# Down stage of an encoder block: x1 and the factor rows in 256 KB pieces, another place for the three-product steps' sum, and a tail by token block

## The chip, the cores and the metric

The kernel runs on one core of one Trainium2 chip. The metric is the device time of one execution in microseconds. Lower is better.

## The reference

One encoder block over 512 tokens and 2048 features, in float32, with a conditioning vector that gives a shift, a scale and a gate for each half:

```
mod = silu(c) @ w_ada + b_ada                    # sh1, sc1, gt1, sh2, sc2, gt2
h = rmsnorm(x, g_norm1) * (1 + sc1) + sh1
x1 = x + gt1 * hybrid_mixer(h, ...)              # mLSTM heads and windowed attention
h = rmsnorm(x1, g_norm2) * (1 + sc2) + sh2
x2 = x1 + gt2 * ((silu(h @ w_gate) * (h @ w_up)) @ w_down)     # FF = 5632
out = rmsnorm(x2, g_final)
```

## The kernel before

Every large product is done as three TensorE passes: a weight tile and an activation tile are each split into an upper part (ScalarE copies it to the rounded type) and a lower part (VectorE subtracts the upper part from the whole), and a product is upper by upper, upper by lower, lower by upper. For each 128x1024 weight tile there is therefore one ScalarE operation, one VectorE operation and 12 matmuls of 512 columns, called an entry. The upper and lower tiles have four buffers (`EHI`, `ELO`), so ScalarE may make the upper part of entry e only when TensorE has finished entry e-4 (`u_used`).

The matrix products of the feed-forward part are done in a seven-product scheme over 2x2 blocks (P1 to P7), which needs sums of weight blocks (VectorE, L1834 in the units, L1975 in the Down stage) and sums of activation blocks.

**The ten middle units.** A unit (u = 1 to 10, 28 entries each) multiplies the next chunk of w_gate and w_up. Beside it the activation of the chunk before is turned by TensorE (`turn_a`), combined by VectorE (`combine_a`, `low_a1`, `low_sums`) and stored to HBM by ScalarE's DMA queue (`turned`, `split_sums`, `keep_sums`, `keep_lows`), to be loaded again in the Down stage: the unsplit parts in `a_keep`, the split pairs in `a_pair`. ScalarE and VectorE work through an order written out by hand: the number in `if e == 14:` is the entry after whose upper or lower part the step stands. TensorE's entry 17 waits for the first four of the middle sums (`middle_y`, L1909, and `middle_zw`, L1918).

**The Down stage.** 44 steps: 11 row chunks of w_down for the near columns' P1, P5, P6, P4 (steps 0 to 10, four products a step), 11 for their P7, P2, P3 (steps 11 to 21, three products), and the same for the other half of the columns (22 to 32, 33 to 43). A step loads 4 or 3 tiles of 512 KB of w_down, 1 MB of pairs (`down_pairs`) and 512 or 256 KB of unsplit blocks (`down_blocks`), all from SyncE's queue. The loads of step s wait for the last lower part of step s-2, the pairs for TensorE's last use of the pairs of step s-2, the blocks for VectorE's `block_lo` of step s-2. `sums_after(e)` says which weight sums stand behind the lower part of entry e on VectorE.

x1, kept in HBM since the middle of the kernel, comes back in pieces (`xp`), is turned by TensorE behind the entries of steps 12 to 19 (`turn_x1`), and copied to `x2`. The gate's factors gt2 are turned to a row (`gain_row`), stored and loaded back for all partitions (`gtb`); `gfb` is the final gain. What the products give is multiplied by the factors and added to x2 (`pre_scale`, `pre_add`, `join_late`, and for the last products `take` and `join_x1`). The tail is the final norm: squares summed by ScalarE (`x2_squares`), mean by VectorE (`final_mean`), power -0.5 by GpSimd (`final_rs`), scaling of half the columns on ScalarE and half on VectorE (`scaled_out`), and four outputs of 1 MB, one for each block of 128 tokens, in the order 2, 3, 0, 1.

Of the kernel before, what the change touches and what calls it, by code (L numbers as in the profile page):

```python
# [34 lines left out]
F32 = mybir.dt.float32  # L35
# [64 lines left out]
def program(nc, x, c, positions, w_ada, b_ada, g1, g2, w_in, b_gates, w_conv, b_conv, gm, sink, ga,  # L100
            w_out, w_gate, w_up, w_down, gf, rope_inv, out, x1_keep, a_keep, a_pair, gt_keep):
    ctx = ExitStack()
    with ctx:
# [142 lines left out]
        gt16 = at("gt16", [KT, P], F32, mix + 28 * S * 4)  # L246
# [57 lines left out]
        sh_ok, sl_ok = gate_sb, gate_sel  # L304
        H0, V0 = 48, 256
# [68 lines left out]
        def sums_after(e):  # L374

            due = [(s, name, FIRST_E[s] + i - 2 + (s == 2) + (s == STEPS - 1))
# [56 lines left out]
        def _(sp):  # L433
# [164 lines left out]
            def x1_piece(cb):  # L598

                if cb >= 2:  # L600
                    sp.wait_ge(xT_ps, 16 + 4 * cb - 4)
                sp.dma_start(xp[cb % 2][:], x1_keep[:, 4 * cb:4 * cb + 4, :]).then_inc(xs_ld[cb % 2], 16)
# [3 lines left out]
            for s in range(STEPS):  # L606
# [23 lines left out]
        def _(pool):  # L630
# [56 lines left out]
            def final_rs(h):  # L687
                pool.wait_ge(n_ms, 1 + h + 1)
                two = slice(2 - 2 * h, 4 - 2 * h)
                pool.tensor_tensor(rs[:, two], ve[:, two], halfneg[:, two], ALU.pow).then_inc(n_rs, 1)  # L690

            final_rs(0)
            final_rs(1)
# [3 lines left out]
        def _(act):  # L697
# [395 lines left out]

            def split_sums(u, rows):

                act.wait_ge(sl_ok, 3 * u - 1)
                act.dma_start(a_pair[rows, 2:8:5, :], a1_lo[:].bitcast(F32)).then_inc(at_st[0], 16)
# [1644 lines left out]
```

## Time and profile before

| | us |
|---|---|
| median of 3 runs (2301.48 to 2304.58) | 2304.0 |
| the profiled execution | 2300.64 |
| its span | 2298.8 |
| TensorE busy, 96% of the span | 2198.7 |
| VectorE busy, 75% | 1729.3 |
| ScalarE busy, 41% | 951.4 |
| GpSimd busy, 9% | 209.3 |

The span is what the trace covers; the execution's own time is 1.8 us above it. Positions below are microseconds from the span's start. The units run from about 1022 to 1812, the Down stage from there to the end. Busy time of TensorE is the time in which a matmul is under way, and matmuls overlap, so a matmul's own duration (0.39 us) is not its pitch.

### The profile page before, as it was taken

To read this page: it belongs to the slowest core of one execution; us is meant where nothing else is said; L and a number is where in the kernel's file an instruction comes from. 1 tells how busy PE (TensorE), PEld (TensorE's weight loads), DVE (VectorE), ACT (ScalarE), POOL (GpSimd) and SP (SyncE) were. 2 spreads that over 40 slices of the span, in tenths; PEclk is the share of its full clock that TensorE was granted. 3 is DMA by queue.
4 is the path that set the end of the run, shared out by engine and by line. 5 is a ranking of instruction groups with operands and counts; after the bars stand their busy time and mean duration, and the time that the engine had idled before them with its cause. 6 is when DMAs were issued, how large, how long until landed. Compare 5 with 4: busy or idle time off the path is not lost.

```text
span 2298.8 us, 27658 instructions
## 1 busy us (share of the span) xinstructions
PE 2198.7 (96%) x10119; PEld 1813.8 (79%) x10119; DVE 1729.3 (75%) x2017; ACT 951.4 (41%) x1231; POOL 209.3 (9%) x72
## 2 busy tenths in 40 slices
PE   5999999999999999999999999999999979999996
PEld 5878878888877788788888888888888768778874
DVE  5978657474766766668887888788888878579976
ACT  4333232323346212454444444444444444455533
POOL 0002333333320013000000000000000000000000
PEclk7999999999999999999999999999999989999998
DMA  9943434344541767225544545544554699999885
GB/s 360 379 155 120 166 129 156 139 162 166 183 160 43 274 259 273 92 101 179 170 169 159 174 169 177 173 160 160 173 178 169 251 369 325 333 317 364 309 297 219
DMA packets 219082, 477.60 MB, mean 208 GB/s; under 512 B 14928, under 2 KB 60272, under 8 KB 202864
## 3 DMA queue, kind: packets, MB, share of 16 engines
q1 hardware_dynamic: 200656, 440.06, 54.4%
q10 hardware_dynamic: 18336, 36.33, 4.2%
q8 instruction: 58, 0.95, 0.2%
q14 instruction: 32, 0.26, 0.0%
HBM read 436.22 MB, written 40.12 MB: 207 GB/s over the span
## 4 chain that ended last, share of the span: by engine, by line
PE 69%; DVE 12%; DMA 7%; issue 5%; ACT 4%; SPq 1%; POOL 1%; ACTq 1%; DVEq 0%; POOLq 0%
PE ps L2162 20%; PE ps L2164 20%; PE ps L2163 20%; DMA wraw<-in_w_down 6%; ACT whi L1044 2%; DVE wraw L1975 1%; PE ps L2319 1%; DVE wlo L1964 1%; DVE acc L1322 1%; PE ps L2332 1%; DVE d_hl L2038 1%; PE ps L2330 1%; PE ps L2253 1%; DMA araw<-in_w_ada 1%; DVE wlo L1815 1%
## 5 line engine op out<-in xcount | busy, mean ns | idle before, releaser
L1044 ACT ACTIVATE whi<-wraw 128x1024 fp32r<-128x1024 f32 x200 | 209.5, 1058 | 226.5 <-DVE wraw L1834 155.3
L1815 DVE TENSOR_TENSOR wlo<-wraw,whi 128x1024 fp32r<-128x1024 f32 x200 | 240.4, 1218 | 63.9 <-ACT whi L1044 63.9
L2162 PE MATMUL ps<-whi,d_hl 128*128 128x512 f32 x616 | 243.6, 395 | 30.6 <-DVE wlo L1964 13.7
L2162 PE MATMUL ps<-h_hi,whi 128*128 128x512 f32 x680 | 272.5, 401 | 0.0
L2164 PE MATMUL ps<-h_hi,wlo 128*128 128x512 f32 x680 | 267.4, 393 | 0.0
L2163 PE MATMUL ps<-h_lo,whi 128*128 128x512 f32 x680 | 267.0, 393 | 0.0
L2162 PE MATMUL ps<-whi,sk_hi 128*128 128x512 f32 x640 | 250.7, 392 | 0.0
L2164 PE MATMUL ps<-whi,sk_lo 128*128 128x512 f32 x640 | 249.2, 389 | 0.0
L2163 PE MATMUL ps<-wlo,sk_hi 128*128 128x512 f32 x640 | 249.1, 389 | 0.0
L2164 PE MATMUL ps<-whi,d_hl 128*128 128x512 f32 x616 | 241.3, 392 | 0.0
L2163 PE MATMUL ps<-wlo,d_hl 128*128 128x512 f32 x616 | 241.1, 391 | 0.0
L2162 PE MATMUL ps<-whi,q_hi 128*128 128x512 f32 x572 | 223.7, 391 | 8.6 <-DVE vg L1918 7.5
L2164 PE MATMUL ps<-whi,q_lo 128*128 128x512 f32 x572 | 222.6, 389 | 0.0
L2163 PE MATMUL ps<-wlo,q_hi 128*128 128x512 f32 x572 | 222.6, 389 | 0.0
L652 POOL TENSOR_TENSOR wlo<-wraw,whi 128x2048 fp32r<-128x2048 f32 x34 | 159.3, 4686 | 441.8 <-ACT whi L746 441.8
L746 ACT ACTIVATE whi<-wraw 128x2048 fp32r<-128x2048 f32 x38 | 72.6, 1911 | 247.1 <-PE ps L2164 247.1
L2162 PEld LDWEIGHTS ps<-whi,d_hl 128*128 128x128 f32 x616 | 116.5, 189 | 60.6 <-issue 21.3
L1559 DVE SCALAR_TENSOR_TENSOR acc<-araw,csil,acc 128x2048 f32<-128x2048 f32 x60 | 159.6, 2660 | 5.1 <-DMA araw<-in_w_ada 2.8
L1044 ACT ACTIVATE whi<-araw 128x1024 fp32r<-128x1024 f32 x80 | 84.7, 1059 | 180.6 <-DVE araw L1834 155.7
L1159 ACT ACTIVATE whi<-wraw 128x1024 fp32r<-128x1024 f32 x88 | 93.2, 1060 | 157.0 <-DVE wraw L1975 99.1
L2164 PEld LDWEIGHTS ps<-h_hi,wlo 128*128 128x128 f32 x680 | 129.0, 190 | 27.5
L2162 PEld LDWEIGHTS ps<-h_hi,whi 128*128 128x128 f32 x680 | 129.7, 191 | 26.1 <-issue 0.8
(363 smaller groups left out, 4120.8 us busy)
## 6 DMA issues: line engine op xcount, KB each, us to landing
araw<-in_w_ada SPq DMA_DIRECT2D x64, 1024.0 KB, 6.2
wraw<-in_w_gate SPq DMA_DIRECT2D x88, 512.0 KB, 3.9
wraw<-in_w_up SPq DMA_DIRECT2D x88, 512.0 KB, 4.7
wraw<-in_w_down SPq DMA_DIRECT2D x88, 512.0 KB, 5.8
d_hl<-a_pair SPq DMA_DIRECT2D x44, 1024.0 KB, 9.2
wraw<-in_w_in SPq DMA_DIRECT2D x38, 1024.0 KB, 5.3
acc<-in_w_down SPq DMA_DIRECT2D x44, 512.0 KB, 7.2
acc<-in_w_up SPq DMA_DIRECT2D x40, 512.0 KB, 5.5
```

The source lines that it names most:

```text
L652: pool.tensor_tensor(xlo[par][:], xraw[par][:], xhi[par][:].bitcast(F32), ALU.subtract)\
L746: A(xhi[par][:], xraw[par][:], ACT.Copy).then_inc(whi_ok, 1)
L1044: A(EHI[e % 4], src, ACT.Copy).then_inc(uhi_ok, 1)
L1159: A(EHI[e % 4], DRAW[s % 2][D_RAW[name]], ACT.Copy).then_inc(uhi_ok, 1)
L1322: V_.scalar_tensor_tensor(out=acc[:, half], in0=slot, scalar=csil[:, kt:kt + 1], in1=acc[:, half], op0=ALU.mult, op1=ALU.add).then_inc(ada ...
L1559: V_.scalar_tensor_tensor(out=acc[:], in0=araw[par][:], scalar=csil[:, kt:kt + 1], in1=acc[:], op0=ALU.mult, op1=ALU.add).then_inc(ada_acc, 1)
L1815: V_.tensor_tensor(ELO[e % 4], src, EHI[e % 4].bitcast(F32), ALU.subtract).then_inc(ulo_ok, 1)
L1964: V_.tensor_tensor(ELO[e % 4], DRAW[s % 2][D_RAW[name]], EHI[e % 4].bitcast(F32), ALU.subtract)\
L1975: V_.tensor_tensor(DRAW[s % 2][i], DRAW[s % 2][i], other, ALU.add).then_inc(usum_ok, 1)
L2162: pe.matmul(o, w_hi, m_hi, start=first, stop=False)
L2163: pe.matmul(o, w_hi, m_lo, start=False, stop=False)
L2164: return pe.matmul(o, w_lo, m_hi, start=False, stop=last)
```

## The change

1. **x1.** The four 1 MB pieces become 16 tiles of 256 KB, spread over the steps (`X1_AT`), with three `xp` buffers in place of two.
2. **Factor row and final gain.** The factors are stored straight from `mod` by ScalarE's queue, ahead of the first unit, column by column; TensorE's transpose and ScalarE's copy (`gain_row`) go. Both rows are loaded in quarters over the steps (`GT_AT`, `GF_AT`).
3. **Three-product steps.** The sum for P7 stands one entry later, behind the last lower part of the step before. The last two steps' order is P7, P7, P2, P2, P3, P3 in place of P7, P2, P7, P2, P3, P3.
4. **Units.** `split_sums` stands behind entry 13 in place of 14, without the store of a1's lower part; that store (`keep_low_a1`) and `keep_sums` stand behind entry 14, `keep_lows` behind 15 in place of 16, and `low_sums` on VectorE behind 14 in place of 15.
5. **Tail.** Joins, mean, power and scaling go by token block; two scalings stand between the joins. The gains of the first half (`gain`) stand in steps 32 to 35 in place of 39 to 42. `block_lo(0)` stands behind the first sums.

```diff
@@ buffers and semaphores
-        xp = [at(f"xp{i}", [P, 4, S], F32, mix + i * 8192) for i in range(2)]
+        xp = [at(f"xp{i}", [P, 4, S], F32, mix + o) for i, o in enumerate((0, 8192, 49152))]
+        x1_ld = [(xs_ld[0], 32), (xs_ld[1], 32), (ada_ld[0], 224), (ada_ld[1], 224)]
@@ down_order, sums_after
-                return [(s + i, p) for ps_ in (("P7", "P2"), ("P3",)) for i in range(2) for p in ps_] if s == STEPS - 2 else []
+                return [(s + i, p) for ps_ in (("P7",), ("P2",), ("P3",)) for i in range(2) for p in ps_] if s == STEPS - 2 else []
-            due = [(s, name, FIRST_E[s] + i - 2 + (s == 2) + (s == STEPS - 1))
+            due = [(s, name, FIRST_E[s] + i - 2 + (s == 2) + down_step(s)[1])
@@ sync
+            def x1_tile(kt):
+
+                cb, (ready, _) = kt // 4, x1_ld[kt // 4]
+                if kt == 12:
+                    sp.wait_ge(xT_ps, 16 + 4)
+                sp.dma_start(xp[cb % 3][:, kt % 4, :], x1_keep[:, kt, :]).then_inc(ready, 16)
+
+            def rows_of(dst, row, ready, quarter):
+
+                part = slice(quarter * S, quarter * S + S)
+                sp.dma_start(dst[:, part], row[part].partition_broadcast(P)).then_inc(ready, 16)
+
+            X1_AT = {2: (0,), 3: (1,), 4: (2, 3), 5: (4,), 6: (5,), 7: (6, 7), 8: (8,), 9: (9,), 10: (10, 11),
+                     16: (12, 13), 17: (14, 15)}
+            GT_AT, GF_AT = (11, 12, 22, 23), (24, 25, 26, 27)
...
                     sp.wait_ge(u_used, 28 * NU)
-                    sp.dma_start(gfb[:], gf.partition_broadcast(P)).then_inc(x_ld[0], 16)
-                    x1_piece(0)
-                    x1_piece(1)
-                if s == NCH + 4:
+                for kt in X1_AT.get(s, ()):
+                    x1_tile(kt)
+                if s in GT_AT:
                     sp.wait_ge(c_ld, 16 + 16)
-                    sp.dma_start(gtb[:], gt_keep.rearrange("a b -> (a b)").partition_broadcast(P)).then_inc(wg_ld, 16)
-                    x1_piece(2)
-                if s == NCH + 6:
-                    x1_piece(3)
+                    rows_of(gtb, gains_row, wg_ld, GT_AT.index(s))
+                if s in GF_AT:
+                    rows_of(gfb, gf, x_ld[0], GF_AT.index(s))
@@ scalar, the units
                         if e == 13:
                             keep_x(u)
+                            split_sums(u, rows)
                         if e == 14:
-                            split_sums(u, rows)
+                            keep_low_a1(u, rows)
+                            keep_sums(u, rows)
                         if e == 15:
-                            keep_sums(u, rows)
-                        if e == 16:
                             keep_lows(u, rows)
 
+            act.wait_ge(modp_ok, 8)
+            act.dma_start(gt_keep.rearrange("a b -> b a"), mod[:, 5, :], allow_slow_non_contiguous=True).then_inc(c_ld, 16)
             unit(1, slice(0, P))
@@ scalar, the tail
+            square(2, 2, 5, 8)
+            square(2, 3, 6, 9)
+            square(3, 2, 7, 10)
+            square(3, 3, 8, 11)
+            scaled_out(0, 2)
+            square(0, 2, 9, 12)
+            scaled_out(1, 3)
+            square(1, 2, 10, 13)
+            square(0, 3, 11, 14)
+            square(1, 3, 12, 15)
+            scaled_out(2, 0)
+            scaled_out(3, 1)
@@ vector, the units
-                        if e == 15:
+                        if e == 14:
                             low_sums(u)
@@ vector, the Down stage and the tail
-                    if e == FIRST_E[3 * NCH + 6 + i]:
+                    if e == FIRST_E[2 * NCH + 10 + i]:
                         gain(i)
...
+            take(0, 0, 1)
+            take(1, 0, 2)
+            take(0, 1, 3)
+            final_mean(2, 2)
+            take(1, 1, 4)
+            dve.wait_ge(x_ld[0], 16 + 64)
+            scaled_out(0, 2)
+            take(2, 0, 5)
+            final_mean(3, 4)
+            take(2, 1, 6)
+            scaled_out(1, 3)
+            take(3, 0, 7)
+            take(3, 1, 8)
+            final_mean(0, 7)
+            final_mean(1, 8)
+            scaled_out(2, 0)
+            scaled_out(3, 1)
@@ tensor
-            def gain_row():
-
-                pe.wait_ge(mix_ok, 6)
-                pe.transpose(ps[6][0:KT, 0:P], mod[:, 5, :], ident[:]).then_inc(cst_T, 1)
-
```

In the new tail `take(i, b, n)` multiplies one block's 512 columns out of PSUM by the factors and adds them to x2 (two VectorE operations), and `square`, `final_mean` and `final_rs` take one block.

## Rows read from the trace of the kernel before

**Rows 1.** TensorE's waits, units (1040 to 1812): line waited for, us in total, times, longest.

```profile
PE ps L2162 <- DVE vg L1918: 7.5, 9, 1.3
```

**Rows 2.** TensorE's waits, Down stage (1790 to 2299).

```profile
PE ps L2162 <- DVE wlo L1964: 13.7, 10, 2.4
PE ps L2162 <- DVE d_hl L2038: 12.6, 1, 12.6
PE ps L2162 <- DMA d_hl<-a_pair: 2.1, 1, 2.1
```

**Rows 3.** Windows: length, busy of PE, PEld, DVE, ACT, POOL, PEclk, DMA share, GB/s.

```profile
1858.00:1862.00 4.00, 3.96 (x9) 3.17 (x10) 4.00 (x4) 0.00 (x0) 0.00 (x0) 0.50 0.93 316
2080.00:2140.00 60.00, 60.00 (x266) 49.71 (x265) 58.61 (x53) 33.19 (x41) 0.00 (x0) 1.00 0.96 356
2210.00:2260.00 50.00, 42.96 (x184) 34.10 (x185) 34.45 (x33) 18.69 (x22) 0.00 (x0) 1.00 0.86 293
```

**Rows 4.** Timeline of VectorE, 1846 to 1858: start, us, engine, line, operation.

```profile
1848.25 0.68 DVE L1864 TENSOR_TENSOR s_lo<-sA,vg_hi 128x512 fp32r<-128x512 f32 x1
1855.62 1.22 DVE L1975 TENSOR_TENSOR wraw<-wraw 128x1024 f32<-128x1024 f32 x1 [6.69 <-DMA wraw<-in_w_down]
```

**Rows 5.** Timeline of TensorE, 1858 to 1862.

```profile
1858.04 0.80 PE L2162 MATMUL ps<-whi,d_hl 128*128 128x512 f32 x1 [12.61 <-DVE d_hl L2038]
```

**Rows 6.** DMA view, 1826 to 1860.

```profile
DMA packets 4456, 12.69 MB, mean 373 GB/s; under 512 B 335, under 2 KB 335, under 8 KB 3817
```

**Rows 7.** Timeline of ScalarE, 1815 to 1866.

```profile
1842.81 0.64 ACT L1100 ACTIVATE vg_hi<-stT 128x512 fp32r<-128x512 f32 x1 [7.16 <-DMA a_pair<-vg_hi]
```

**Rows 8.** Chain that ended last, 2239 to 2250: start, us, what.

```profile
2239.89 6.58 DMA wraw<-in_w_down
...
2246.57 1.23 DVE wraw L1975
2247.80 0.60 DVE d_hl L2038
2248.40 1.14 DVE wlo L1964
```

**Rows 9.** DMA issues of the whole span: count, KB each, median us to landing.

```profile
out<-x SPq DMA_DIRECT2D x4, 1024.0 KB, 6.3
...
wgraw<-in_w_in SPq DMA_DIRECT2D x1, 128.0 KB, 7.6
```

**Rows 10.** Timeline of TensorE, its last matmul.

```profile
2280.48 0.39 PE L2164 MATMUL ps<-whi,d_hl 128*128 128x512 f32 x1
```

**Rows 11.** Timeline of VectorE, the tail.

```profile
2283.35 0.69 DVE L2079 TENSOR_TENSOR x<-x,c 128x512 f32<-128x512 f32 x1
...
2285.10 4.87 DVE L2092 SCALAR_TENSOR_TENSOR x<-x,tiny,gfb 128x1024 f32<-128x1024 f32 x4
```

**Rows 12.** Timeline of SyncE, the tail.

```profile
2286.47 4.11 SPq L625 DMA_DIRECT2D out<-x  x4
```

**Rows 13.** Timeline of ScalarE, one unit (1205 to 1240), entries 14 to 16.

```profile
1212.20 1.06 ACT L1044 ACTIVATE whi<-araw 128x1024 fp32r<-128x1024 f32 x1 [0.69 <-PE ps L2164]
...
1215.49 0.63 ACT L1100 ACTIVATE vg_hi<-stT 128x512 fp32r<-128x512 f32 x1 [2.23 <-DVE a_lo L1856]
...
1217.37 1.06 ACT L1044 ACTIVATE whi<-wraw 128x1024 fp32r<-128x1024 f32 x1 [0.72 <-ACT vg_hi L1101]
...
1221.54 0.34 ACTq L1109 DMA_DIRECT2D a_pair<-s_lo  x1
```

**Rows 14.** Timeline of VectorE, the same unit.

```profile
1213.56 1.22 DVE L1856 TENSOR_TENSOR a_lo<-stT,vg_hi 128x1024 fp32r<-128x1024 f32 x1
...
1218.46 1.23 DVE L1815 TENSOR_TENSOR wlo<-wraw,whi 128x1024 fp32r<-128x1024 f32 x1 [2.54 <-ACT whi L1044]
...
1220.81 1.22 DVE L1815 TENSOR_TENSOR wlo<-wraw,whi 128x1024 fp32r<-128x1024 f32 x1
...
1227.76 1.28 DVE L1918 TENSOR_TENSOR vg<-ps,u2b 128x512 f32<-128x512 f32 x2
```

**Rows 15.** Timeline of TensorE, the same unit, entry 17.

```profile
1229.17 0.49 PE L2162 MATMUL ps<-whi,q_hi 128*128 128x512 f32 x1 [0.78 <-DVE vg L1918]
```

More of the change, by code:

```diff
@@ L685, in _, with final_rs @@
             pool.tensor_tensor(rs, ve, halfneg, ALU.pow).then_inc(n_rs, 1)
[L687 to L693, printed above, removed]
+            def final_rs(n, tb):
+                pool.wait_ge(n_ms, 1 + n + 1)
+                pool.tensor_tensor(rs[:, tb:tb + 1], ve[:, tb:tb + 1], halfneg[:, tb:tb + 1], ALU.pow).then_inc(n_rs, 1)
+            for n, tb in enumerate((2, 3, 0, 1)):
+                final_rs(n, tb)
         @block.scalar
@@ L1190, in x1_turned, with square, x2_squares, scaled_out @@
                 A(x2[:, g % 4, g // 4 * S:(g // 4 + 1) * S], ps[6 + g % 2][:], ACT.Copy).then_inc(xT_sb, 1)
-            def x2_squares(n, i, halves=(0, 1)):
-                h, c = ((1, 0), (1, 1), (0, 0), (0, 1))[i]
-                for b in halves:
-                    act.wait_ge(x2_ok, 4 * n + i + 1 + (b if n and i == 3 else 0))
-                    if n or i or b:
-                        act.wait_ge(ssq_ok, TB + 8 * n + 2 * i + b)
-                    tb, cb = 2 * h + b, 2 * n + c
-                    A(vg[:, 0, :], x2[:, tb, cb * S:(cb + 1) * S], ACT.Square, accum_out=ssq4[:, tb, cb:cb + 1])\
-                        .then_inc(ssq_ok, 1)
-            def scaled_out(h):
-                act.wait_ge(n_rs, 1 + h + 1)
+            def square(tb, cb, ready, done):
+                act.wait_ge(x2_ok, ready)
+                if done:
+                    act.wait_ge(ssq_ok, TB + done)
+                A(vg[:, 0, :], x2[:, tb, cb * S:(cb + 1) * S], ACT.Square, accum_out=ssq4[:, tb, cb:cb + 1])\
+                    .then_inc(ssq_ok, 1)
+            def x2_squares(i):
+                h, c = ((1, 0), (1, 1), (0, 0), (0, 1))[i]
+                for b in range(2):
+                    square(2 * h + b, c, i + 1, 2 * i + b)
+            def scaled_out(n, tb):
+                act.wait_ge(n_rs, 1 + n + 1)
                 act.wait_ge(z_ok, 4)
-                for tb in (2 - 2 * h, 3 - 2 * h):
-                    A(x2[:, tb, 0:2 * S], x2[:, tb, 0:2 * S], ACT.Copy, scale=rs[:, tb:tb + 1]).then_inc(y_ok[0], 1)
+                A(x2[:, tb, 0:2 * S], x2[:, tb, 0:2 * S], ACT.Copy, scale=rs[:, tb:tb + 1]).then_inc(y_ok[0], 1)
             block_hi(0)
@@ L1224, in _ @@
                 if e == 10:
+                    keep_low_a1(NCH, slice(NU * P, NCH * P))
                     keep_sums(NCH, slice(NU * P, NCH * P))
@@ L1243, in _ @@
                     if e == END_E[2 * NCH + 2 * i + 2]:
-                        x2_squares(0, i)
-            for i in range(3):
-                x2_squares(1, i)
-            x2_squares(1, 3)
-            scaled_out(0)
-            scaled_out(1)
+                        x2_squares(i)
+            square(2, 2, 5, 8)
[10 more added lines that the diff above has]
+            scaled_out(3, 1)
         @block.vector
@@ L2054, in gain, with take @@
                 if i == 0:
-                    dve.wait_ge(x_ld[0], 16 + 16)
+                    dve.wait_ge(x_ld[0], 16 + 32)
                 V_.tensor_tensor(x2_part(0, h, c), x2_part(0, h, c), both(gfb[:, c * S:(c + 1) * S]), ALU.mult)\
                     .then_inc(z_ok, 1)
-            def take(i, b=None):
+            def take(i, b, n):
                 name, c, t = (("P7", 0, tmp[0]), ("P7", 1, tmp[1]), ("P2", 0, kept), ("P3", 1, left))[i]
-                if b is None:
-                    dve.wait_ge(u_used, E0 + end_of(1, name))
-                    if i == 0:
-                        dve.wait_ge(pre_ok, 14)
-                for k in (range(2) if b is None else (b,)):
-                    last = V_.tensor_tensor(t[:, k, :], ps[DBANK[1][name] + k][:], gains(1, c), ALU.mult)
-                last.then_inc(t_ok, 1)
@@ L2088, in scaled_out @@
-            def scaled_out(h):
-                dve.wait_ge(n_rs, 1 + h + 1)
-                for tb in (2 - 2 * h, 3 - 2 * h):
-                    V_.scalar_tensor_tensor(out=x2[:, tb, 2 * S:], in0=x2[:, tb, 2 * S:], scalar=rs[:, tb:tb + 1],
-                                            in1=gfb[:, 2 * S:], op0=ALU.mult, op1=ALU.mult).then_inc(y_ok[1], 1)
-            block_lo(0)
+                dve.wait_ge(u_used, E0 + end_of(1, name) + (b if name == "P3" else 0))
+                V_.tensor_tensor(t[:, b, :], ps[DBANK[1][name] + b][:], gains(1, c), ALU.mult).then_inc(t_ok, 1)
```

69 lines of the change are left out of this document (22 added, 47 removed).

## Prediction

> **What bounds the kernel now.** I read the waits of TensorE first, because it is the engine that works nearly all the time, and split them at the end of the ten middle units. In the units TensorE waits 7.5 us in nine equal small waits, always for the same VectorE line L1918 [rows 1]. In the Down stage it waits 13.7 us in ten pieces for lower weight parts (L1964), once 12.6 us for a block's lower part (L2038), and once 2.1 us for a transfer of pairs [rows 2]. Next the windows: the four-product stretch has no idle time at all, with the DMA engines 0.96 busy; the second three-product stretch loses 7 of 50 us [rows 3]. 60 us for 266 matmuls gives 2.71 us for an entry of 12 matmuls: 10.85 us for a four-product step, 8.1 us for a three-product step. So TensorE bounds the kernel, and only an added or removed wait of TensorE, or the tail after it, can move the time. The timelines then say how each wait comes about.
>
> **The start of the Down stage: about 7.5 us less.** At step 2 SyncE queues the final gain and two x1 pieces, 3 x 1.05 MB, ahead of step 3's loads. VectorE, free at 1848.9, waits until 1855.6 for those loads (first sum of step 3), and L2038, which stands behind that sum in VectorE's order, releases TensorE at 1858.0 [rows 4, 5]. The change leaves 0.26 MB there: 2.88 MB less at the 373 GB/s of this stretch [rows 6] is 7.7 us. But VectorE can't be earlier than 1848.9, so the wait falls by 6.7 us. It doesn't go to nothing: ScalarE stood 7.2 us for its own store until 1842.8 [rows 7], VectorE's place follows from that, and the store still shares the DMA engines. Should the store land sooner, up to 3 us more come back; should it hold all up, 3 us less. After the long wait TensorE restarts at a granted clock of 0.50, the lower of its two levels (1.2 GHz): 9 matmuls in 4 us, where full clock gives 17.7 at 266 in 60 us [rows 3]; the 8.7 that lack are 2.0 us. I count 0.8 us of that as saved (0 to 2). Range 4 to 11.
>
> Afterwards the pieces must fit into the steps. A four-product step loads 3.67 MB (9.8 us at 373 GB/s, of 10.85): 1.0 us is free, a piece takes 0.7 us. Two pieces in one step (steps 4, 7, 10) take 1.4 us and lean on the next one. The factor and gain rows, one quarter a step, go by the same sum. I count 0.
>
> Here the Trainium skill speaks against the change: "DMA: Bandwidth & Descriptors", section Bandwidth, Measured, says to batch DMAs to 1 MiB or more and gives 2.0 us plus bytes over 436 GB/s each. By it 18 more transfers cost 36 us of DMA time. The trace agrees only for a transfer that stands alone; queued 512 KB loads moved at 373 GB/s in the mean. By the row the sum has 0 for it.
>
> **Three-product steps: 13.7 us less.** The chain there is a loop: load 6.58 us, sum 1.23 us, block's lower part 0.60, lower part of the last product 1.15, issue of the next load: 9.6 to 10 us for a step of 8.1 [rows 8]. The cause is that the sum of step s+1 stands ahead of the last lower part of step s, which releases the loads of s+2. With the sum behind it, the loads go out about one landing earlier. The new loop: after the last lower part come sum 1.2, upper part 1.1 and lower part 1.15 us, against a need three entries later; about 4 us of room. Bandwidth: 2.88 MB a step is 7.7 us at 373 GB/s, under 8.1. So all ten waits [rows 2] go. Bound: if bandwidth holds at two thirds, 9 us. VectorE gets the gains of L2056 in steps 32 to 35 too, beside the mixing; step 33 then holds some 10 us of its work against 8.1, with about 5 us of lead before it. I take 0, bound 2 us of loss.
>
> **The last two steps: 1.1 us less.** Both P7 now go first, so step 43's pairs are needed two entries (5.4 us) after they are issued, before three. A 1 MB transfer alone lands in 6.3 us [rows 9]; now they stand behind late loads, then they will not. Wait 1.0 in place of 2.1 us; bounds 0 and 4. The gain row's transpose and its TensorE wait disappear, 0.3 us.
>
> **The tail: 1.9 us less.** Now TensorE ends at 2280.9 and the span at 2298.8, 17.9 us [rows 10]. VectorE ends its joins 3.2 us after TensorE, and then four scalings take 4.87 us [rows 11]; the four outputs are issued from 2286.5 to 2290.6 and 4.2 MB drain in a row [rows 12]. After: from the last P7 until TensorE's end are 10.9 us; VectorE starts its block work 2.4 us into them (last upper and lower part) and has 16 half operations of 0.69, two scalings of 1.2 and two means of 0.35: free 5.5 us after TensorE. Square 0.85, mean 0.35, power up to 1.7, last scaling 1.2: last output issued 9.6 us after TensorE, landing 6.3 us later: 16.0 us. Blocks 2 and 3 are out by then. Bounds 0 and 4.
>
> **The ten units: 17.4 us more.** The diff also moves three things in every unit, which its name doesn't tell. Follow one unit. Now: the upper part of entry 14 starts at 1212.20, right when TensorE allows; then ScalarE waits for L1856 (1213.56, ends 1214.8), issues a store, makes two copies from 1215.49 and starts entry 15's upper part at 1217.37 [rows 13]. Its lower part is at 1218.46, the two sums' lower parts behind it, entry 16's lower part at 1220.81, and from there without a gap the weight sum, entry 17, the middle sums, L1918 at 1227.76 [rows 14]; TensorE starts entry 17 at 1229.17, 0.78 late [rows 15]. After: the copies stand between entry 13 and 14. They still need L1856 (the buffer is shared), so ScalarE stands until 1214.9, and entry 14's upper part starts 1.88 us (1217.37 less 1215.49) later, 1216.8. Its lower part: 1.09 us later, 1217.9. The sums' lower parts now stand behind it, until 1220.25 (2.35 from one part to the next but one, as 1218.46 to 1220.81). ScalarE must see these before it issues the last two stores, which stand ahead of entry 16's upper part. The stores now end at 1221.9, 1.07 us behind their release, then 0.2: entry 16's upper part at 1221.5, its lower part at 1222.6. That is 1.8 us later than 1220.81, and all that follows is back to back up to L1918. TensorE's own time doesn't move, so the wait is 0.78 + 1.8 = 2.6 us. Entries 14 to 16 themselves are due at 1220.3, 1223.0 and 1225.7 (2.71 each before 1228.4) and have their lower parts by 1219.1, 1221.4 and 1223.7. Nine waits of 0.83 become 2.6: 15.9 us; unit 1 has none now and some room, 1.5 us. The queues passed: three stores of 0.5 us stand ahead of entry 15's upper part, in its room. Bounds: 0, if the stores cost ScalarE nothing and the order resolves itself; 22, if entry 16 is late as well.
>
> **The factor row's store.** It goes out column by column, 2048 single values, ahead of unit 1, where ScalarE waits for its first load anyway. The nearest row has 2048 runs of 64 bytes: 7.6 us to landing among other loads [rows 9]. It may delay the first loads of unit 1. TensorE is there still busy with the entries of the stage before. I take 0, bound 3 us. The same page of the Trainium skill (section Latency and other measured facts) says that a last dimension that isn't contiguous gives one descriptor per element; no run here shows its price for 4 bytes.
>
> **Sum.** -7.5 - 13.7 - 1.1 - 0.3 - 1.9 + 17.4 = -7.1 us: 2293.5 against the profiled execution's 2300.6, whose span is 2298.8. The median of the runs is 2304.0, 3.4 us above it, so 2296.9 on the scale of the runs.
>
> **Rivals.** (a) The units don't slow: ScalarE's issue of stores overlaps, entry 16 is in time. Then -24.5: 2279.5. For it: the stores' own landing is close to L1918 as well and gets 0.5 us earlier. Against: each dependency above is written in the code. (b) The three-product steps stay bound by transfers: 355 GB/s wanted against 373. The ten waits stay or shift to the pairs: +6.6, 2310. Against: 0.96 busy without a wait in the four-product stretch [rows 3]. (c) Each small piece costs the DMA engines a fixed time: 6.3 us for 1 MB less 2.8 us of moving is 3.5 us. 12 pieces in steps 2 to 10 are 42 us against 9 free: +33, less 7: about 2330. It decides from 1.0 us a piece on. Its rule is the page's rule on batching. (d) The wait at the start remains, since ScalarE's store and not the queue holds it: -0.4: 2303.6.
>
> **How the numbers follow.** Forecast 0.60 (its own range 2290 to 2303), (a) 0.15, (b) 0.12, (c) 0.05, (d) 0.08. A measurement tells 0.2%, 4.6 us, from no change: faster is below 2299.4, slower above 2308.6. Of the forecast's 0.60, 0.43 are faster, 0.15 within, 0.02 slower; (a) is faster; (b) 0.05 within and 0.07 slower; (c) slower; (d) 0.06 within, 0.01 each side. Faster 0.59, same 0.26, slower 0.15. The range 2284 to 2307 leaves out most of (a), and (c) with a part of (b).
>
> **What would show it.** The wait for L1918 should read about 2.6 us in each unit and each unit 1.8 us longer. The wait for L2038 should be near 6 us, those for L1964 in the Down stage gone, the tail near 16 us, and the DMA share in the three-product steps above 0.9. A unit wait still at 0.8, or waits for loads in steps 4 to 10, makes the prediction wrong.

## The result, and the profile after

| | before | after |
|---|---|---|
| median of 13 runs each, in turns on one chip | 2303.6 us (2297.9 to 2307.7) | 2310.3 us (2305.0 to 2316.5) |
| ratio, 95% interval | | 1.0031 (1.0021 to 1.0041) |
| profiled execution | 2300.6 us | 2313.3 us |
| its span | 2298.8 us | 2311.5 us |
| its mean granted clock | 0.979 | 0.976 |

The forecast was 2296.9 us and faster; the kernel is slower, by 6.7 us in the medians and outside the range of 2284 to 2307. The two profiled executions lie 12.7 us apart, because before's is 3 us under its median and after's 3 us over. The sums below are made between these two executions; what a single edit is worth on the scale of the runs is read from the experiments.

TensorE's waits after the change, in the ten units (1040 to 1832) and in the Down stage (1800 to 2312), answer to [rows 1] and [rows 2]. The first view:

```profile
PE ps L2167 <- DVE vg L1933: 25.0, 10, 2.6
```

The second:

```profile
PE ps L2167 <- DVE d_hl L2053: 4.2, 1, 4.2
...
PE ps L2167 <- DMA d_hl<-a_pair: 2.0, 1, 2.0
```

L1933 is L1918 of before, L2053 is L2038. The unit waits have grown from 7.5 to 25.0 us. In the Down stage the long wait has gone from 12.6 to 4.2 us, and the ten waits for L1964 are no longer there. The wait for the pairs is what it was.

Windows of after (columns as in [rows 3]). The first lies in the three-product steps, the second is the start of entry 17 in one unit:

```profile
2210.00:2260.00 50.00, 49.99 (x220) 40.98 (x220) 41.27 (x39) 20.23 (x25) 0.00 (x0) 1.00 0.95 337
...
1245.00:1249.00 4.00, 3.89 (x10) 3.09 (x11) 4.00 (x6) 0.00 (x0) 0.00 (x0) 0.57 0.78 258
```

The Down stage does what was forecast: 220 matmuls in 50 us where before had 184, at a DMA share of 0.95. The second window is what the forecast lacked. TensorE is busy for 3.89 of 4 us and starts only ten matmuls, since the granted clock is 0.57 there, next to the lower of its two levels. In before the same place had the full clock. Window of before:

```profile
1229.00:1233.00 4.00, 3.83 (x17) 3.17 (x18) 4.00 (x7) 0.00 (x0) 0.00 (x0) 1.00 0.73 260
```

**One unit, followed as in the prediction.** Timeline of ScalarE in after, entries 14 to 16 (answers to [rows 13]):

```profile
1229.06 0.64 ACT L1113 ACTIVATE vg_hi<-stT 128x512 fp32r<-128x512 f32 x1 [3.46 <-DVE a_lo L1871]
...
1230.93 1.06 ACT L1053 ACTIVATE whi<-araw 128x1024 fp32r<-128x1024 f32 x1 [0.72 <-ACT vg_hi L1114]
...
1233.62 1.06 ACT L1053 ACTIVATE whi<-wraw 128x1024 fp32r<-128x1024 f32 x1 [1.63 <-issue]
...
1235.11 0.35 ACTq L1122 DMA_DIRECT2D a_pair<-s_lo  x1
1235.65 1.06 ACT L1053 ACTIVATE whi<-wraw 128x1024 fp32r<-128x1024 f32 x1 [0.96 <-issue]
```

Timeline of VectorE (to [rows 14]):

```profile
1232.03 1.22 DVE L1830 TENSOR_TENSOR wlo<-araw,whi 128x1024 fp32r<-128x1024 f32 x1 [3.14 <-ACT whi L1053]
...
1236.74 1.22 DVE L1830 TENSOR_TENSOR wlo<-wraw,whi 128x1024 fp32r<-128x1024 f32 x1 [0.80 <-ACT whi L1053]
...
1243.70 1.28 DVE L1933 TENSOR_TENSOR vg<-ps,u2b 128x512 f32<-128x512 f32 x2
```

Timeline of TensorE at entry 17 (to [rows 15]):

```profile
1245.11 0.49 PE L2167 MATMUL ps<-whi,q_hi 128*128 128x512 f32 x1 [2.62 <-DVE vg L1933]
...
1247.06 0.63 PE L2169 MATMUL ps<-whi,q_lo 128*128 128x512 f32 x1
1247.48 0.63 PE L2167 MATMUL ps<-whi,q_hi 128*128 128x512 f32 x1
...
1249.54 0.39 PE L2167 MATMUL ps<-whi,sk_hi 128*128 128x512 f32 x1
1249.77 0.39 PE L2168 MATMUL ps<-wlo,sk_hi 128*128 128x512 f32 x1
```

ScalarE stands for L1871, makes the copies, and only then entry 14's upper part. From the lower part of entry 14 to that of entry 16 it is 4.71 us (1232.03 to 1236.74), as forecast (4.7), and from there to L1933 6.96 us, as before (6.95). So the wait is 2.62, as forecast. But behind it the matmuls start 0.43 us apart (1247.06, 1247.48) in place of 0.23 (1249.54, 1249.77), until 1248.8. Against the full clock's pitch the seven whole pitches of that kind lose 1.4 us here, and two partly slow ones beside them 0.2. From this entry 17 to that of the next unit (1327.58) it is 82.47 us; in before a unit takes 79.03 (1229.17 to 1308.22 and on). 1.84 of the 3.44 us are the longer wait and 1.6 the clock. The lower clock stood behind all nine waits of 2.6 us, twice for double the length (2.96 us lost), and behind none of before's nine, nor behind unit 1's wait of 1.34. In all it cost 16.5 us (17.0 with every partly slow pitch counted).

**The start of unit 1.** DMA view of after, 1005 to 1040: the queue of the factor row's store (packets, MB, share of the 16 DMA engines) and its issue (as in [rows 9]):

```profile
q10 hardware_dynamic: 2064, 0.01, 2.6%
...
gt_keep<-mod ACTq DMA_DIRECT2D x1, 8.0 KB, 11.4
```

The same view for 1009 to 1012 and for 1018 to 1021, in which the store has not landed yet (q1 is the queue of the loads):

```profile
q10 hardware_dynamic: 2064, 0.01, 30.7%
```

```profile
q1 hardware_dynamic: 54, 0.11, 71.5%
```

Timelines of SyncE, of ScalarE and of TensorE in after:

```profile
1013.19 2.51 SPq L550 DMA_DIRECT2D wraw<-in_w_gate  x1
1015.74 5.06 SPq L550 DMA_DIRECT2D wraw<-in_w_up  x1
```

```profile
1023.31 1.06 ACT L1053 ACTIVATE whi<-wraw 128x1024 fp32r<-128x1024 f32 x1 [12.95 <-DMA wraw<-in_w_gate]
```

```profile
1030.36 0.80 PE L2167 MATMUL ps<-whi,q_hi 128*128 128x512 f32 x1 [7.68 <-DVE wlo L1830]
```

And TensorE's start of unit 1 in before:

```profile
1022.51 0.50 PE L2162 MATMUL ps<-whi,q_hi 128*128 128x512 f32 x1 [1.18 <-ACT mg L1052]
```

The 8 KB land 11.4 us after their issue. All 2064 packets of the store are recorded within 1009 to 1012. What is slow until it lands are the loads behind it: from 1018 to 1021 they are the only packets in the view, 54 of them take 0.72 of the DMA engines' time for 0.11 MB, 37 GB/s. What holds them is not shown. SyncE is held for 2.5 and 5.1 us at two issues; unit 1's first load lands only at 1023.3, and TensorE waits 7.68 us where it waited 1.18 before. The clock behind the wait costs another 1.8 us: 8.3 in all.

**The tail.** Timelines of TensorE, of SyncE and of VectorE in after (to [rows 10] to [rows 12]):

```profile
2296.74 0.39 PE L2169 MATMUL ps<-whi,d_hl 128*128 128x512 f32 x1
```

```profile
2296.26 10.57 SPq L634 DMA_DIRECT2D out<-x  x4
```

```profile
2305.14 1.29 DVE L2093 SCALAR_TENSOR_TENSOR x<-x,tiny,gfb 128x1024 f32<-128x1024 f32 x1 [0.44 <-POOL tiny L699]
```

TensorE's end is at 2297.1, and the span's is 14.4 us later, 17.9 before. The last scaling ends 9.3 us after TensorE (forecast: 9.6), and three outputs are on their way by then. The outputs of 1 MB, now apart from each other, land 3.9 us after their issue in the median and 4.6 at most, where the four in a row of before took 6.3 [rows 9].

Together: 8.3 (start of unit 1) + 17.5 (unit waits) + 16.5 (clock behind them) is 42.3 us, and where the Down stage begins TensorE is 44.1 us later than before. Of the 1.8 between them 1.4 lie ahead of unit 1 (TensorE reaches its wait there at 1022.68, in before at 1021.33). At the stage's end it is 16.3 us later, so 27.8 have come back there, and 3.5 come back in the tail. That leaves the difference of the spans, 12.7.

### The profile page after: what moved, and what is told of

It is laid out like the page before. It is cut to its first block, busy times and chain, and to the rows that moved or that the text cites. A ratio compares the mean times of both kernels' runs of the same rounds, so it can differ in the third digit from the quotient of the medians.

```text
span 2311.5 us, 27684 instructions
## 1 busy us (share of the span) xinstructions
PE 2211.5 (96%) x10118; PEld 1824.2 (79%) x10118; DVE 1734.9 (75%) x2024; ACT 953.0 (41%) x1230; POOL 210.1 (9%) x74
## 4 chain that ended last, share of the span: by engine, by line
PE 71%; DVE 11%; issue 6%; ACT 5%; DMA 3%; ACTq 2%; POOL 1%; SPq 0%; DVEq 0%; POOLq 0%
PE ps L2167 21%; PE ps L2168 21%; PE ps L2169 21%; ACT whi L1053 2%; PE ps L2324 1%; DMA araw<-in_w_ada 1%; DVE wlo L1979 1%; DVE acc L1337 1%; DMA wraw<-in_w_down 1%; DMA fr<-in_w_ada 1%; PE ps L2337 1%; PE ps L2335 1%; DVE araw L1849 1%; DVE vg L1933 1%; DVE wraw L1990 1%
## 5 line engine op out<-in xcount | busy, mean ns | idle before, releaser
L1053 ACT ACTIVATE whi<-wraw 128x1024 fp32r<-128x1024 f32 x200 | 209.5, 1058 | 262.4 <-DVE wraw L1849 149.4
L2167 PE MATMUL ps<-whi,q_hi 128*128 128x512 f32 x572 | 230.9, 404 | 32.7 <-DVE vg L1933 25.0
L2168 PE MATMUL ps<-wlo,q_hi 128*128 128x512 f32 x572 | 229.7, 402 | 0.0
L2169 PE MATMUL ps<-whi,q_lo 128*128 128x512 f32 x572 | 229.2, 401 | 0.0
L1830 DVE TENSOR_TENSOR wlo<-araw,whi 128x1024 fp32r<-128x1024 f32 x80 | 97.8, 1223 | 90.4 <-ACT whi L1053 90.4
L2167 PEld LDWEIGHTS ps<-whi,q_hi 128*128 128x128 f32 x572 | 111.3, 195 | 60.6 <-issue 27.4
```

The costliest lines, as they stand in the source:

```text
L1053: A(EHI[e % 4], src, ACT.Copy).then_inc(uhi_ok, 1)
L1830: V_.tensor_tensor(ELO[e % 4], src, EHI[e % 4].bitcast(F32), ALU.subtract).then_inc(ulo_ok, 1)
L2167: pe.matmul(o, w_hi, m_hi, start=first, stop=False)
L2168: pe.matmul(o, w_hi, m_lo, start=False, stop=False)
L2169: return pe.matmul(o, w_lo, m_hi, start=False, stop=last)
```

## The experiments

The account that they test, A in the expectations, is the one just given: the units' new order costs its waits and the lower clock behind them, the row's store costs its wait, and what the name of the change tells of is a gain. The rivals stand in each expectation. Each run's median has its ratio to before, with the interval, behind it. The e, f and g runs were made in three sets on three chips, each with before beside them (medians 2303.8, 2304.6 and 2302.2 us). Between sets the difference of two medians and that of two ratios can lie 3 us apart, and a ratio's interval is 3 to 5 us wide on either side.

**The two suspects taken out of the changed kernel.** e1 puts the units' order back:

```diff
                         if e == 13:
                             keep_x(u)
-                            split_sums(u, rows)
                         if e == 14:
                             keep_low_a1(u, rows)
-                            keep_sums(u, rows)
+                            split_sums(u, rows)
                         if e == 15:
-                            keep_lows(u, rows)
+                            keep_sums(u, rows)
+                        if e == 16:
+                            keep_lows(u, rows)
...
-                        if e == 14:
+                        if e == 15:
                             low_sums(u)
```

e2 only moves the factor row's store behind unit 1, and e3 does both:

```diff
-            act.wait_ge(modp_ok, 8)
-            act.dma_start(gt_keep.rearrange("a b -> b a"), mod[:, 5, :], ...).then_inc(c_ld, 16)
             unit(1, slice(0, P))
+            act.wait_ge(modp_ok, 8)
+            act.dma_start(gt_keep.rearrange("a b -> b a"), mod[:, 5, :], ...).then_inc(c_ld, 16)
```

> The changed kernel with the order of before in the ten units: the two copies and the stores of the sums stand behind entries 14, 15 and 16 again, the sums' lower parts behind 15. Theory A (the units' new order costs its wait of 2.6 us in place of 0.8 and, through the wait, a stretch at the lower clock in every unit): the ten waits for the middle sum fall from 25.0 to some 8 us, the stretches at the lower clock in the units go, the profiled span is 17.5 + 16.5 = 34 us shorter than the changed kernel's, about 2278. Rival B (the lower clock in the units is not the wait's doing): only 17.5 us come back, 2294. The wait of 7.7 us at the start of unit 1 stays in either case.

> The changed kernel with the column-wise store of the factors moved behind unit 1, 79 us later. Theory A (2048 writes of 4 bytes hold the DMA engines for some 9 us, and the first loads of unit 1 stood behind them): the 7.7 us wait at the start of unit 1 falls to 1.2, with the 1.8 us of lower clock behind it, 8 us in all; the store now meets loads that are issued a step ahead, and costs 0 to 3 us there. Rival B (the loads of unit 1 are late for another reason, the new order or the position of ScalarE): the wait stays. Rival C: the store costs the same 8 us in its new place.

> The changed kernel with both: the order of before in the units, and the store of the factors behind unit 1. If the two costs are separate they add: 34 + 8 = 42 us less than the changed kernel's span of 2311.5, about 2270, and some 29 us less than the kernel before (ratio 0.987), which is what the Down stage and the tail give. If the gains of the Down stage needed the slower units, it is nearer to 2285.

Measured: e1 2280.8 us, 0.9901 (0.9887 to 0.9915); e2 2303.1, 1.0006 (0.9994 to 1.0018); e3 2273.8, 0.9876 (0.9861 to 0.9891). The order of the units costs 29.5 us (after to e1) or 29.3 (e2 to e3), the store 7.2 (after to e2) or 7.0 (e1 to e3). So 7 us is what the old place costs more than the new one. In e2 the store lands in 12.2 us, and there too it holds SyncE, for 3.4 us at one issue. e3 shows what follows. Timelines of SyncE, of ScalarE and of TensorE in e3, behind the store and at entry 17 of unit 2:

```profile
1094.68 3.01 SPq L550 DMA_DIRECT2D wraw<-in_w_up  x1
```

```profile
1106.08 1.06 ACT L1053 ACTIVATE whi<-wraw 128x1024 fp32r<-128x1024 f32 x1 [3.75 <-DMA wraw<-in_w_gate]
```

```profile
1152.82 0.49 PE L2168 MATMUL ps<-whi,q_hi 128*128 128x512 f32 x1 [1.96 <-DVE vg L1934]
```

ScalarE waits for a late load, VectorE waits 0.9 us for ScalarE's copy of it, and TensorE's wait in unit 2 is 1.96 us where the units after it have 0.80, with 1.6 us of lower clock behind it. All six kernels with the old order and the store in this place (e3, f2, f4, g1, g2, g3) have such a wait in unit 2, of 1.8 to 2.2 us, and the lower clock behind it. Before has 1.27 there and e1 1.64, without the lower clock. In e2 it is 3.33 us in place of 2.6. A store of this kind is not free there either. e2's unit waits are 25.6 us in all, near the 25.0 of after, but the lower clock follows six of its nine waits of 2.6 us or more, with 10.7 us lost. TensorE's waits in the units of e3:

```profile
PE ps L2168 <- DVE vg L1934: 8.3, 9, 2.0
```

**The units' order alone, in the kernel before.** g4 makes only the moves of split_sums, keep_low_a1, keep_sums, keep_lows and low_sums there, e1's diff the other way.

> The kernel before with the three moves in the units alone. Theory A (their price doesn't depend on the rest of the change): ten waits of 2.6 us in place of nine of 0.8, and the lower clock behind most of them; 25 to 34 us slower, ratio 1.011 to 1.015. Rival B (the lower clock comes only with the rest of the change): 17.5 us slower, 1.008.

2329.9 us, 1.0125 (1.0105 to 1.0145): 27.8 us more. Its waits in the units:

```profile
PE ps L2167 <- DVE vg L1923: 24.9, 10, 2.6
```

They are 17.4 us more than [rows 1] has, which is to the digit what the prediction said of the order. Another 9.3 us went to the lower clock, behind six of the nine waits of 2.6 us (the tenth, in unit 1, is 1.34).

**The clock apart from the wait.** e4 is the changed kernel with nine more matmuls where TensorE waits in the unit; their result is used by nothing, and the waits for data stay.

```diff
                         elif e == 17:
+                            pe.wait_ge(ulo_ok, 28 * u - 28 + (e + 1))
+                            pe.wait_ge(mid_ok, 8 * u - 6)
+                            for _ in range(9):
+                                pe.matmul(ps[6][:], a_block("P4", 0, 0)[0], EHI[e % 4][:, 0:S], start=True, stop=True)
                             pe.wait_ge(mid_ok, 8 * u - 4)
```

> The changed kernel with nine more matmuls in every unit, into a free bank, ahead of entry 17 while TensorE waits for the middle sum: 2.0 us of work inside a wait of 2.6 us, the release is the same. The extra products are not used. Theory A (it is the idle time that lowers the granted clock): the stretches at the lower clock behind the waits go, 16.5 us less, with the ten releases at the same distance; span about 2295. Rival B (the clock falls for another reason, a budget of activity for example): more work makes it no better, 2311 or longer.

2298.5 us, 0.9976 (0.9966 to 0.9986): 11.9 us less than after, with 90 matmuls more. TensorE's waits in its units, and the window around entry 17:

```profile
PE ps L2643 <- DVE u2b L1924: 2.0, 9, 0.2
```

```profile
1230.00:1250.00 20.00, 19.79 (x86) 15.73 (x85) 15.43 (x18) 7.05 (x7) 0.00 (x0) 1.00 0.60 210
```

The wait itself isn't mended: the data come as late, and the time is filled. A unit takes 80.81 us, 1.6 less than one of after with the lower clock once, and 3.0 less than one with it for double the length; no unit has it here. That the clock, and not some other price of the order, is the second term is thereby shown.

**Part of the order.** f3 is e3 with split_sums alone behind entry 13; the low parts and the stores stay where they were.

```diff
                         if e == 13:
                             keep_x(u)
+                            split_sums(u, rows)
                         if e == 14:
                             keep_low_a1(u, rows)
-                            split_sums(u, rows)
```

> e3 with one of the three moves in the units alone: the two copies (split_sums) behind entry 13, all stores of sums and lower parts and VectorE's low_sums where the kernel before has them. Theory A (the copies ahead of entry 14's upper part delay the whole chain; by my working the three paths end within 0.1 us of each other): the wait for the middle sum is 2.4 to 2.6 us in each unit, the lower clock comes back, some 30 us above e3, about 2304. Rival B (the last two stores ahead of entry 16's upper part make it): the wait stays at 0.8 to 1.0 us, within 3 us of e3.

2281.3 us, 0.9891 (0.9874 to 0.9907), and its waits in the units:

```profile
PE ps L2168 <- DVE vg L1934: 13.6, 10, 2.2
```

The expectation (waits of 2.4 to 2.6) missed. The copies alone make them 1.38 us; a unit takes 79.65 us, so 0.6 us more than before's 79.03, and the lower clock follows only the one of 2.18. The lower parts of entries 14 and 16 are 3.48 us apart there, 1.23 less than in after. That is the two low sums' share together with the stores ahead of entries 15 and 16; no run parts the two. Ahead of each of those upper parts ScalarE stood on issuing in after (1.63 and 0.96 us in the timeline above). f3 is 7.5 us above e3 by the medians and 3.5 by the ratios. The rows of the units give 5.3 of it (13.6 against 8.3), and at step 43 its TensorE waits 2.6 us for a lower part, with the lower clock behind, where e3 waits 1.7 for the pairs. So the copies alone are the smaller part of the 29.5 us; the rest, 22 us or more, comes with the other moves and with the clock.

**The sum behind the last lower part, alone, in the kernel before.** f1 is one line:

```diff
-            due = [(s, name, FIRST_E[s] + i - 2 + (s == 2) + (s == STEPS - 1))
+            due = [(s, name, FIRST_E[s] + i - 2 + (s == 2) + down_step(s)[1])
```

> The kernel before with one line of the change alone: the sum of a three-product step one entry later, behind the last lower part of the step before. Theory A (that order alone makes the loop of load, sum and lower part): nine or ten of the ten waits for lower parts (13.7 us) go, with 1.4 us of lower clock behind the longest; 13 to 15 us faster, ratio 0.994. Rival B (the loop needed the transfers of x1 and the factor row out of the way too): only the five or six waits of steps 35 to 42 go, 7 us. Rival C (transfers bind): under 3 us, the waits show up as waits for loads or pairs.

2281.9 us, 0.9893 (0.9877 to 0.9909): 22.6 us less by the medians, where 13 to 15 were expected. All ten waits for L1964 are gone, and the wait for the pairs with them. The wait of 12.0 us at the start of the stage is still there. TensorE's waits from 1790 on, and a window of the three-product steps:

```profile
PE ps L2162 <- DVE d_hl L2038: 12.0, 1, 12.0
```

```profile
2190.00:2240.00 50.00, 50.00 (x222) 41.44 (x221) 41.70 (x39) 21.44 (x24) 0.00 (x0) 1.00 0.99 353
```

The same window of before:

```profile
2190.00:2240.00 50.00, 45.25 (x197) 36.28 (x196) 36.38 (x35) 18.59 (x22) 0.00 (x0) 1.00 0.86 291
```

The transfers could do more than they were asked for: 353 GB/s without a wait, against 291 with one in each step. Rival (b) of the prediction falls.

The gain is larger than the waits' 13.7 us. The pairs' wait adds 2.1. Each wait also costs more than its row says. Timeline of TensorE in before, around the wait of [rows 15]:

```profile
1228.01 0.39 PE L2164 MATMUL ps<-whi,q_lo 128*128 128x512 f32 x1
...
1229.50 0.39 PE L2163 MATMUL ps<-wlo,q_hi 128*128 128x512 f32 x1
```

From the last start before the wait (1228.01) to the second behind it (1229.50) are 1.49 us, where two pitches are 0.45: 1.04 us are lost by a wait whose row says 0.78. Eleven times 0.25 is 2.8 us more. Last, the longest of the ten, 2.4 us, had seven matmuls wholly at the lower clock behind it, 1.4 us. That makes 20 us. The spans of the two profiled executions are 17.4 apart, but f1's reached unit 1 5.3 us later (1027.77, before 1022.51), in a part that the edit doesn't touch; from there on they are 22.7 apart. The medians are 22.6 apart, with an interval of 21 to 28 from the ratio. About 1 us of what is between are smaller rows: 0.5 in unit 2's wait, 0.6 in the long wait and 0.5 in the tail, less 0.6 of lower clock behind the long wait. The rest stays open.

**The small pieces, queued together again.** f2 is e3 with the same pieces, all of them in the steps where before had its large ones:

```diff
-            X1_AT = {2: (0,), 3: (1,), 4: (2, 3), 5: (4,), 6: (5,), 7: (6, 7), 8: (8,), 9: (9,), 10: (10, 11),
-                     16: (12, 13), 17: (14, 15)}
-            GT_AT, GF_AT = (11, 12, 22, 23), (24, 25, 26, 27)
+            X1_AT = {2: tuple(range(8)), 15: tuple(range(8, 12)), 17: tuple(range(12, 16))}
+            GT_AT, GF_AT = (15,), (2,)
```

> The changed kernel with the order of before in the units and the store of the factors behind unit 1 (e3), but with the 256 KB pieces of x1, gain and factor row queued together at the steps of before (2, 15, 17). Theory A (what counts is how many bytes stand ahead of the loads, not the pieces' size): the wait at step 2 is 12.6 us again in place of 3.9, with up to 2 us of lower clock, and the rest stays: 9 to 11 us above e3, about 2284. Rival B (ScalarE's wait for its own store sets the restart): 0 to 3 us above e3. Rival C (small pieces are what helps): as e3.

2284.3 us, 0.9907 (0.9891 to 0.9922), 10.5 more than e3 by the medians and 7 by the ratios; the two profiled spans are 10.8 apart. TensorE's longest wait from 1790 on:

```profile
PE ps L2169 <- DVE d_hl L2055: 13.7, 1, 13.7
```

The wait is 9.8 us longer than e3's 3.9, and the pairs are waited for twice, 3.0 us in all against 1.7. So the place of the pieces is worth some 10 us (7 to 10.5). Their size costs nothing that shows. Window of e3 over steps that carry pieces:

```profile
1860.00:1950.00 90.00, 90.00 (x399) 74.55 (x398) 76.93 (x69) 42.13 (x42) 0.00 (x0) 1.00 0.99 375
```

399 matmuls in 90 us is the pitch of the stretch without a wait in [rows 3], at 375 GB/s, and from the end of the long wait to step 43 TensorE waits for nothing.

**What holds the rest of the start.** In after, ScalarE stands for its own store, as the prediction's rival (d) had it, and then VectorE's order follows. Timelines of ScalarE and VectorE in after:

```profile
1885.21 0.63 ACT L1113 ACTIVATE vg_hi<-stT 128x512 fp32r<-128x512 f32 x1 [5.50 <-DMA a_pair<-vg_hi]
```

```profile
1891.27 1.22 DVE L1990 TENSOR_TENSOR wraw<-wraw 128x1024 f32<-128x1024 f32 x1
1892.40 1.22 DVE L2053 TENSOR_TENSOR d_hl<-d_raw,d_hl 128x1024 fp32r<-128x1024 f32 x1
```

f4 is e3 with the block's lower part ahead of the low sums and of the sum:

```diff
+                if e == END_E[0] + 4:
+                    block_lo(2)
                 if e == 10:
                     low_sums(NCH)
...
-                for s in range(2, STEPS):
+                for s in range(3, STEPS):
                     if e == END_E[s - 2] + 4:
                         block_lo(s)
```

> e3 with the block's lower part of step 2 (block_lo(2)) ahead of low_sums and of step 3's first sum in VectorE's order. Theory A (after the change TensorE's wait at step 2 is VectorE's order behind ScalarE's 5.2 us wait for its store, no longer a transfer): the 3.9 us wait falls by 1.14 + 1.2 us to 1.6 us, and with it the 1.55 us of lower clock behind it: 3.8 us less than e3, about 2270. Rival B (transfers still set it): no change.

2272.4 us, 0.9857 (0.9842 to 0.9872). The wait falls from 3.9 to 1.5 us, without a lower clock behind it, but TensorE now comes sooner to the pairs of step 43 and waits 3.2 us for them in place of 1.7, with 1.6 us of clock behind. In the profiled executions most of the gain is given back there, some 380 us later. f4 is 1.4 us below e3 by the medians and 4.4 by the ratios, so the runs don't tell the 3.8 expected from nothing. TensorE's waits in the Down stage of f4:

```profile
PE ps L2170 <- DMA d_hl<-a_pair: 3.2, 1, 3.2
...
PE ps L2170 <- DVE d_hl L2054: 1.5, 1, 1.5
```

**The last steps and the tail.** g1 is e3 with the old order of the last two steps, which asks for the pairs three entries after their issue and not two; g2 is e3 with the old joins, squares, means and scalings (by halves of the blocks, not by block).

```diff
-                return [(s + i, p) for ps_ in (("P7",), ("P2",), ("P3",)) ...
+                return [(s + i, p) for ps_ in (("P7", "P2"), ("P3",)) ...
```

> e3 with the order of before in the last two steps (P7, P2, P7, P2, P3, P3). Theory A (both P7 first puts step 43's pairs one entry nearer to their issue, and gives VectorE its last P7 one entry sooner): the wait for the pairs, 1.7 us in e3, goes to 0 to 0.5, and the tail grows by 0 to 2 us, since VectorE and not TensorE ends the tail; within 2 us of e3. Rival B (the new order is what shortens the tail): 2 to 4 us slower than e3.

> e3 with the tail of before (joins of two blocks at a time, all scalings at the end, four outputs in a row). Theory A (the four outputs of 1 MB drain one behind the other, and the new tail sends two of them off earlier): from TensorE's last matmul to the end 17 to 18 us again in place of 14.4; 2 to 4 us slower than e3. Rival B (the last block's output sets the end in either): within 1 us of e3.

g1 took 2271.8 us, 0.9868 (0.985 to 0.9886); g2 2273.8, 0.9876 (0.9856 to 0.9895). Neither can be told from e3. In g1 the wait for step 43's pairs is gone (1.7 us in e3); its one wait of 0.9 us for pairs, at 2216, is some 30 us earlier. g2's tail is 15.9 us long and g1's 14.9, e3's 14.4 and before's 17.9. So the work by block is worth 1.5 us with the new order of the last steps and 3.1 with the old one, and the order 2.0 or 0.4: the two overlap. g2's median is e3's to 0.01 us, which is chance, since they are from different sets; its interval holds the 2 to 4 us expected of it as well as nothing. The tail's row got shorter, and the runs can't show what that is worth.

**Both mends together.** g3 is f4 with the last steps' old order, so e3, the block first, and the pairs with three entries of room.

> The candidate for the fastest: e3, block_lo(2) ahead of low_sums and the first sum, and the last two steps in the order of before. Each took or should take a wait of TensorE: 2.4 us with 1.5 us of lower clock at step 2, and 1.7 to 3.2 us of pairs with 1.6 us of lower clock at step 43. If both hold, 3 to 6 us below e3, ratio 0.985 or less.

2269.4 us (2269.0 to 2269.8), 0.9856 (0.9835 to 0.9877): 32.8 us less than before, and the lowest median of the case; against e3 it is 4.4 us lower, f4 and g1 lie between. The wait for the pairs is gone, the block's is 1.9 us.

## Why the prediction was wrong

The step that failed is **"The ten units: 17.4 us more"**, which sized the wait and not what follows it. The wait was right (2.62 us for 2.6, 25.0 in all; 24.9 when the order was put alone into before). The term left out is the granted clock behind it: 16.5 us in the profiled execution, and some 10 to 12 in the medians (27.8 by g4 and 29.5 by e1, less 17.4 of waits). The prediction knew the effect, since it took 2.0 us for it behind the wait of 12.6 us, where the granted clock read 0.50 [rows 3], and the waits for L1964 held a case at 2.4 us too. It didn't ask the question again for ten waits that it was about to make 2.6 us long. e4 shows the term by itself. The Trainium skill ("TensorE: Matmul & The Clock Gate", Part 1: The HAM clock gate) puts the penalty of the ramp at under 1% of a typical kernel's span. It says so of the warm-up at a kernel's start; the stretches behind these nine waits, in the middle of a busy kernel, are 0.7% of the span. The trace agrees with the size, and 0.7% was more than the whole change was worth.

**The factor row's store** was the second miss: 0 with a bound of 3 us, measured 7.0 and 7.2 against the store behind unit 1, and 8.3 in the profiled execution. The row it was priced by, 2048 runs of 64 bytes landing in 7.6 us [rows 9], was a transfer on which nothing waited. The landing was not so far off (11.4), but the argument that TensorE was still busy was: ScalarE had waited for the loads that now stood behind this store, and TensorE's cover was shorter than the delay. The Trainium skill's rule on a last dimension that isn't contiguous, one descriptor per element ("DMA: Bandwidth & Descriptors", Rules for kernel authors, and not the section that the prediction names), which the sum went without, is one with which the trace agrees: the store's queue shows 2064 packets for 0.01 MB.

**Three-product steps:** the mechanism was right, the size too small. 13.7 us were forecast, and the line alone gives 22.6. The 0.25 us behind each wait, the pairs' wait and a case of the lower clock are the main parts that could be named.

**The start of the Down stage:** 7.5 us forecast; the wait fell by 8.4 and the place of the pieces is worth 7 to 10.5 by f2, within the step's range of 4 to 11. Rival (d), that ScalarE's store holds the wait, can be true only of the 4 us that remain: ScalarE waits 5.5 us for its store there, VectorE's order alone makes 2.4 of them by f4, and no run takes the store's wait away. The rival's price in the prediction has the wrong sign: -7.1 + 7.5 is 0.4 us more, 2304.4.

**The pieces in the steps:** 0, and 0 measured. Rival (c) is not seen: in a queue that other loads keep full the pieces cost no measurable time. Nor is its row what the prediction took it for. The 6.3 us of [rows 9] are four outputs issued in a row; apart from each other they landed in 3.9 in after. The Trainium skill's rule on batching to 1 MiB or more ("DMA: Bandwidth & Descriptors", Bandwidth, Measured) does not show in these steps either; the fixed 2.0 us, by which the prediction estimated 36 us for 18 more transfers, stands in the same page's section on the anatomy of one DMA.

**The last two steps:** the pairs' wait is 2.0 us for a forecast of 1.0, and with the old order (g1, g3) there is none at step 43. The new order gave the pairs less room; the runs show no gain from it. **The tail:** 14.4 us for a forecast of 16.0, most of it in the landing (3.9 to 4.6 us for 6.3), and no effect that the runs can show.

**Rival (a)**, the units don't slow, fell with the first row of waits. Its time, 2279.5, is close to e1's 2280.8, though for its own reasons: there the Down stage's larger gain and the store's cost nearly cancel.

Set side by side on the scale of the runs: -22.6 (the sum's place), -10.5 (the pieces' place, -7 by the ratios), 0 (tail and last order, not told by the runs), +29.5 (units), +7.2 (store) is +3.6 against a measured +6.7, 3 us apart, which is the size of what such sums of medians from different sets leave.

## What to carry to other kernels

A new wait on the busiest engine has two prices, its row and what the engine's clock does behind it; look in the trace for a wait of that length and read the granted clock of the stretch after it, before the sum is made. A diff's small moves deserve the same working as its headline: here a few lines moved in a loop of ten took back most of what the headline brought (29.5 us of some 33), and one store the rest. And a store of single values is priced by what is queued behind it, since the other queue's loads came late behind it in both of its places: 7.7 us of waiting where they were needed next, about 1 us where they had a lead.

## What the runs showed of the hardware

- A transfer of 8 KB in 2048 pieces of 4 bytes took 11.4 to 12.6 us to landing (after, e1 to e3, f2 to f4, g1 to g3). Its own packets were recorded in the first 3 us; behind them the loads of another engine's queue moved at 37 GB/s with a DMA share of 0.72, and single issues of that queue took 2.5 and 5.1 us (after), 3.4 (e2) and 3.0 (e3).
- In kernels where TensorE is otherwise busy, waits of 2.6 us had the lower level of the clock (1.2 GHz) behind them in 9 of 9 cases in after and in 6 of 9 in g4; the matmuls then start 0.43 us apart for 6 to 8 of them, or twice as many. Waits of 0.8 us (eight in before) and of 1.38 us (eight in f3) had none. Between 1.7 and 3.3 us both occur: 1.96 in e3 had it and 3.33 in e2 had not, so the length of one wait doesn't decide it.
- A wait costs TensorE about 0.25 us more than its row: 0.15 until the first matmul starts, 0.10 at the second.
- 256 KB pieces among other loads brought no wait: 375 GB/s at a DMA share of 0.99 in e3, with TensorE at its full pitch.
